# The first transfers of a two-layer transformer trunk, taken in fourths and in turn, with ScalarE as a second issuer

## The reference, cut to what matters

```python
def rmsnorm(x, g):
    y = x * lax.rsqrt(jnp.mean(x * x, axis=-1, keepdims=True) + EPS)
    return y * g

def swiglu(h, w_gate, w_up, w_down):
    return (jax.nn.silu(h @ w_gate) * (h @ w_up)) @ w_down

for i in range(DEPTH):                       # DEPTH = 2
    x = x + 0.5 * swiglu(rmsnorm(x, norm_ff1[i]), ff1_w_gate[i], ff1_w_up[i], ff1_w_down[i])
    x = x + token_mixer(rmsnorm(x, norm_mix[i]), ...)
    x = x + 0.5 * swiglu(rmsnorm(x, norm_ff2[i]), ff2_w_gate[i], ff2_w_up[i], ff2_w_down[i])
    g = jax.nn.sigmoid(rmsnorm(x, norm_ple[i]) @ ple_w_gate[i])
    x = x + g * (p[i] @ ple_w_proj[i])
return rmsnorm(x, norm_final)
```

## Time and profile before

| | |
|---|---|
| median of 3 runs | 1175.71 us (1175.65 to 1175.8) |
| the profiled execution's own time | 1175.59 us |
| its span, from the first to the last instruction | 1173.7 us |
| TensorE busy | 1166.6 us, 99% of the span |
| VectorE, ScalarE, GpSimd busy | 820.7, 609.7, 117.1 us |
| DMA | 218.87 MB, mean 186 GB/s |

### The profile page before, as it was taken

The page is one execution under the profiler, slowest core; times in us unless marked ns, Lnnn a source line. Parts: engine busy times, 40 slices in busy tenths (PEclk is TensorE's granted clock), DMA queues, the critical chain, the costliest instruction groups (busy, mean ns, idle before and its releaser), DMA issues.

```text
span 1173.7 us, 24027 instructions
## 1 busy us (share of the span) xinstructions
PE 1166.6 (99%) x10518; PEld 1142.9 (97%) x10518; DVE 820.7 (70%) x936; ACT 609.7 (52%) x688; POOL 117.1 (10%) x130
## 2 busy tenths in 40 slices
PE   9999999999999999999999999999999999999998
PEld 9999999999999999999999999999899999999998
DVE  6866545697978766655786665458799787666556
ACT  6544445555745644444764443446466555444445
POOL 2000001011512000001110000100134020000011
PEclk9999999999999999999999999999999999999999
DMA  8655555545445555555556555554644456555551
GB/s 294 232 202 190 189 206 169 193 150 200 154 145 194 200 193 201 192 187 198 191 175 224 183 203 189 183 214 140 220 145 146 143 204 211 205 182 202 192 180 37
DMA packets 33528, 218.87 MB, mean 186 GB/s; under 512 B 5200, under 2 KB 6544, under 8 KB 7440
## 3 DMA queue, kind: packets, MB, share of 16 engines
q1 hardware_dynamic: 32992, 216.82, 53.3%
q10 hardware_dynamic: 432, 0.52, 0.1%
HBM read 216.15 MB, written 1.05 MB: 185 GB/s over the span
## 4 chain that ended last, share of the span: by engine, by line
PE 98%; DMA 1%; DVE 1%; ACT 0%; SPq 0%; issue 0%; DVEq 0%
PE psum L409 32%; PE psum L410 31%; PE psum L411 31%; PE psum L691 1%; PE psum L670 1%; DMA x_all<-in_x 1%; PE psum L543 0%; PE psum L604 0%; PE psum L654 0%; PE psum L725 0%; DVE gates L1801 0%; PE psum L736 0%; PE psum L639 0%; PE psum L759 0%; DVE hB_lo L1769 0%; PE psum L586 0%
## 5 line engine op out<-in xcount | busy, mean ns | idle before, releaser
L1309 DVE TENSOR_TENSOR w_lo<-raw,w_hi 128x2048 fp32r<-128x2048 f32 x200 | 457.9, 2292 | 218.2 <-ACT w_hi L905 218.0
L905 ACT ACTIVATE w_hi<-raw 128x2048 fp32r<-128x2048 f32 x201 | 385.2, 1916 | 352.3 <-PE psum L411 347.7
L409 PE MATMUL psum<-hA_hi,w_hi 128*128 128x256 f32 x1360 | 377.6, 278 | 0.0
L410 PE MATMUL psum<-hA_hi,w_lo 128*128 128x256 f32 x1360 | 375.7, 276 | 0.0
L411 PE MATMUL psum<-hA_lo,w_hi 128*128 128x256 f32 x1360 | 375.7, 276 | 0.0
L409 PEld LDWEIGHTS psum<-hA_hi,w_hi 128*128 128x128 f32 x1360 | 255.4, 188 | 2.7 <-issue 2.7
L410 PEld LDWEIGHTS psum<-hA_hi,w_lo 128*128 128x128 f32 x1360 | 255.4, 188 | 0.0
L411 PEld LDWEIGHTS psum<-hA_lo,w_hi 128*128 128x128 f32 x1360 | 255.3, 188 | 0.0
L409 PE MATMUL psum<-hB_hi,w_hi 128*128 128x256 f32 x832 | 229.9, 276 | 0.6 <-DVE w_lo L1777 0.6
L410 PE MATMUL psum<-hB_hi,w_lo 128*128 128x256 f32 x832 | 229.7, 276 | 0.0
L411 PE MATMUL psum<-hB_lo,w_hi 128*128 128x256 f32 x832 | 229.7, 276 | 0.0
(11 more groups left out here) (207 smaller groups left out, 1241.4 us busy)
## 6 DMA issues: line engine op xcount, KB each, us to landing
raw<-in_weights SPq DMA_DIRECT2D x203, 1024.0 KB, 4.9
raw<-in_weights SPq DMA_DIRECT2D x2, 512.0 KB, 6.3
x_all<-in_x SPq DMA_DIRECT2D x1, 520.0 KB, 3.6
x_all<-in_x SPq DMA_DIRECT2D x1, 512.0 KB, 6.3
relu<-in_p SPq DMA_DIRECT2D x2, 256.0 KB, 5.1
consts<-in_consts SPq DMA_DIRECT2D x1, 384.0 KB, 5.1
out<-gates ACTq DMA_DIRECT2D x2, 192.0 KB, 2.3
out<-gates SPq DMA_DIRECT2D x2, 192.0 KB, 2.3
```

What stands on the lines that cost most here:

```text
L409: pe.matmul(o, lh, rh, start=start, stop=False)
L410: pe.matmul(o, ll, rh, start=False, stop=False)
L905: act.activation(w_hi[:, s, :], raw[:, s, :], ACT.Copy).then_inc(hi_ready[s], 1)
L1309: dve.tensor_tensor(w_lo[:, s, :], raw[:, s, :], w_hi[:, s, :].bitcast(F32), ALU.subtract).then_inc(lo_ready[s], 1)
```

## The change

x is loaded in fourths (two tiles each), and so are chunks 0 and 1; chunk 2 is loaded in halves. SyncE issues x's and chunk 1's fourths in turn, then chunk 2's halves. ScalarE issues the four pieces of chunk 0, ahead of its first activation. All four engines take the fourths in turn: of each fourth first x, then chunk 0's piece, then chunk 1's, and on ScalarE the squares of that pair behind them (of the last fourth behind chunk 2). TensorE takes chunk 0's and chunk 1's fourth m, then m + 1; chunk 2's products run by halves of k, into banks 5 and 6. The sum over the partitions, `mean_everywhere`, moves from ahead of chunk 3's products to behind its first 12. `WARM` goes from 18 to 11. Later FFNs keep their code, moved into `chunks_in_pieces`.

```diff
-X_HALVES = ((0, HEAD_WORDS + 4 * T), (HEAD_WORDS + 4 * T, HEAD_WORDS + 8 * T))
-WARM = 18
+X_FOURTHS = tuple((HEAD_WORDS * (i > 0) + 2 * T * i, HEAD_WORDS + 2 * T * (i + 1)) for i in range(4))
+WARM = 11
...
+            for i in range(4):
+                part = slice(*X_FOURTHS[i])
+                sp.dma_start(x_all[:, part], a["x"][:, part]).then_inc(x_landed[i], 16)
+                sp.dma_start(raw[:, 1, piece(i)], a["weights"][1, :, piece(i)]).then_inc(piece_landed[1][i] if i < 3 else landed[1], 16)
             for i in range(2):
-                part = slice(*X_HALVES[i])
-                sp.dma_start(x_all[:, part], a["x"][:, part]).then_inc(x_landed[i], 16)
                 half = slice(1024 * i, 1024 * i + 1024)
-                sp.dma_start(raw[:, 0, half], a["weights"][0, :, half]).then_inc(landed[0] if i else half_landed, 16)
-            chunk(0, 1)
-            chunk(0, 2)
+                sp.dma_start(raw[:, 2, half], a["weights"][2, :, half]).then_inc(landed[2] if i else half_landed, 16)
...
+                    if q == 3 and L + f == 0:
+                        by_columns(s, b, h, (0,), range(4))
+                        mean_everywhere(L, k, 4)
+                        by_columns(s, b, h, (0,), range(4, 8))
...
+            def first_chunks(h):
+                for m in range(4):
+                    if m < 3:
+                        pe.wait_ge(piece_lo, m + 1)
+                    else:
+                        operands(0, 0)
+                    pe.wait_ge(h_ready, of_norm(0, 0, m + 1))
+                    for c in range(2):
+                        mm = pairs(0, 0, h, c, (2 * m, 2 * m + 1))
+                    if m == 3:
+                        mm.then_inc(chunk_done[0], 1)
+                    if m < 3:
+                        pe.wait_ge(next_lo, m + 1)
+                    else:
+                        operands(0, 1)
+                    for c in range(2):
+                        mm = pairs(1, 2, h, c, (2 * m, 2 * m + 1))
+                mm.then_inc(chunk_done[1], 1)
+
+            def third_chunk(h):
+                for i in range(2):
+                    if i:
+                        operands(0, 2)
+                    else:
+                        pe.wait_ge(half_lo, 1)
+                    for c in range(2):
+                        mm = pairs(2, THIRD_BANKS, h, c, range(4 * i, 4 * i + 4))
+                mm.then_inc(chunk_done[2], 1)
...
+            for i in range(4):
+                act.dma_start(raw[:, 0, piece(i)], a["weights"][0, :, piece(i)]).then_inc(piece_landed[0][i] if i < 3 else landed[0], 16)
             act.wait_ge(half_ready, 1)
             act.activation(rsum[:, 0, :], half_neg[:, 0:2], ACT.Copy)
+            for m in range(4):
+                act.wait_ge(x_landed[m], 16)
+                for c in (2 * m, 2 * m + 1):
+                    ins = act.activation(hB[0][:, c, :], x[:, c, :], ACT.Copy, scale=first_gains[:, c:c + 1])
+                ins.then_inc(h_hi_ready, 1)
+                act.wait_ge(piece_landed[0][m] if m < 3 else landed[0], 16)
+                act.activation(w_hi[:, 0, piece(m)], raw[:, 0, piece(m)], ACT.Copy).then_inc(piece_hi if m < 3 else hi_ready[0], 1)
+                act.wait_ge(piece_landed[1][m] if m < 3 else landed[1], 16)
+                act.activation(w_hi[:, 1, piece(m)], raw[:, 1, piece(m)], ACT.Copy).then_inc(next_hi if m < 3 else hi_ready[1], 1)
+                if m < 3:
+                    squares(0, 0, m)
             for i in range(2):
...
+                half = slice(1024 * i, 1024 * i + 1024)
+                act.wait_ge(landed[2] if i else half_landed, 16)
+                act.activation(w_hi[:, 2, half], raw[:, 2, half], ACT.Copy).then_inc(hi_ready[2] if i else half_hi, 1)
             squares(0, 0, 3)
```

More of the change, by code:

```diff
@@ L224, in hybrid_trunk @@
         masks_landed = sem("masks_landed")
-        x_landed = [sem(f"x_landed{i}") for i in range(2)]
+        x_landed = [sem(f"x_landed{i}") for i in range(4)]
         layer_landed = sem("layer_landed")
@@ L489, in ffn @@
                 mm.then_inc(chunk_done[s], 1)
[L490 to L518, removed]
-                                       hid[0][:, k, :], hid[1][:, k, :], k == 0, k == 21)
-                        if k == 21 and m < 3:
-                            mm.then_inc(acc_ready, 1)
-                    mm.then_inc(chunk_done[s], 1)
+            def first_chunks(h):
[11 more added lines that the diff above has]
+                        pe.wait_ge(next_lo, m + 1)
+                    else:
+                        operands(0, 1)
+                    for c in range(2):
+                        mm = pairs(1, 2, h, c, (2 * m, 2 * m + 1))
+                mm.then_inc(chunk_done[1], 1)
@@ L1383, in ffn @@
                     chunk_products(L, n)
-                    dve.tensor_tensor(gate_sum, products(2 * g), both(rb), ALU.mult).then_inc(gate_scaled, 1)
+                    dve.tensor_tensor(gate_sum, high(THIRD_BANKS) if L + f == 0 and g == 1 else products(2 * g), both(rb), ALU.mult
+                                      ).then_inc(gate_scaled, 1)
                     if g:
@@ L1779, in _ @@
-            for i in range(4):
-                if i < 3:
-                    dve.wait_ge(next_hi, i + 1)
+            for m in range(4):
+                dve.wait_ge(x_landed[m], 16)
+                dve.wait_ge(h_hi_ready, of_norm(0, 0, m + 1))
+                for c in (2 * m, 2 * m + 1):
+                    ins = dve.scalar_tensor_tensor(out=hB[1][:, c, :], in0=x[:, c, :], scalar=first_gains[:, c:c + 1],
+                                                   in1=hB[0][:, c, :].bitcast(F32), op0=ALU.mult, op1=ALU.subtract)
+                ins.then_inc(h_ready, 1)
+                if m < 3:
+                    dve.wait_ge(piece_hi, m + 1)
+                else:
+                    dve.wait_ge(hi_ready[0], 1)
+                dve.tensor_tensor(w_lo[:, 0, piece(m)], raw[:, 0, piece(m)], w_hi[:, 0, piece(m)].bitcast(F32), ALU.subtract
+                                  ).then_inc(piece_lo if m < 3 else lo_ready[0], 1)
+                if m < 3:
+                    dve.wait_ge(next_hi, m + 1)
@@ L1782, in _ @@
                 else:
                     dve.wait_ge(hi_ready[1], 1)
-                next_piece(i)
-            split(0, 2)
+                next_piece(m)
+            for i in range(2):
+                half = slice(1024 * i, 1024 * i + 1024)
+                if i:
+                    dve.wait_ge(hi_ready[2], 1)
+                else:
+                    dve.wait_ge(half_hi, 1)
+                dve.tensor_tensor(w_lo[:, 2, half], raw[:, 2, half], w_hi[:, 2, half].bitcast(F32), ALU.subtract
+                                  ).then_inc(lo_ready[2] if i else half_lo, 1)
```

77 lines of the change are left out of this document (44 added, 33 removed).

## The result

The changed kernel takes 1177.30 us, the median of 22 runs (1176.34 to 1179.05), against 1175.72 for the kernel before (22 runs, 1175.41 to 1176.04). The ratio is 1.0014, with a 95% interval from 1.0008 to 1.0020. The forecast was 1174.7 with a range of 1173.5 to 1176.5: the sign was wrong and the time lies outside. By the bound of the prediction (0.2%, 2.35 us) the difference of 1.58 counts as within, the case that had 0.89. But the spread is new: before the runs lie within 0.6 us, after within 2.7. One execution of all that follow, the profiled one of experiment 5, ran at a granted clock of 0.75 throughout and took 1459.58 us; its time is left out everywhere.

What follows compares the result with a forecast made beforehand. TensorE bounds the kernel, busy 1166.6 of 1173.7 us. A start 0.83 earlier and gaps of 0.32 and 0.30 gone, against 0.5 of new wait and 0.1 for rounding, were put near 1.0 less: 1174.7 us, range 1173.5 to 1176.5.

Steps and rivals of the forecast that it cites:

- the case that had 0.89: Whole kernel: the time stays within 0.2% (2.35 us) of the kernel before, chance 0.89.
- its own 0.5 of waiting: Ahead of chunk 3: TensorE, free at 23.7, waits 0.5 us for `w_lo`, ready at 24.15.
- 0.83, 0.32 and 0.30 less 0.5 and 0.1: Whole sum: 0.83 earlier start, gaps of 0.32 and 0.30 gone, less 0.5 new wait and 0.1 for rounding over chunk 5.
- the chain at chunk 3: Chunk 3: load out at 15.05, landed 19.95, split 24.15, first product 24.2; 1.09 us gained at the chunk's end.
- ScalarE's four issues: Kernel start: four load issues ahead of the table load cost ScalarE 1.8 us, 2.8 at the dear end.
- I cost the supply at nothing, hidden behind ScalarE: Chunks 0 and 1: x's fourths land before ScalarE asks, so transfers add nothing; TensorE runs from 7.2 to 23.7.
- rival (a): Kernel start: ScalarE isn't held up by its issues; first product at 6.2, chunk 3 at 23.2, 1173.7 us; chance 0.14.
- The pace of the fourths: Chunks 0 and 1: per fourth TensorE needs 2.75 us, ScalarE 2.61, VectorE 2.13; chunk 0 is split at 14.95.
- Rival (c): Chunks 0, 1 and 3: fourths starved at 215 GB/s, chunk 0 done 3.15 later; 1177.8 us, 1178.7 with dear issues; chance 0.12.
- rival (b): First products: idle behind the shorter warm-up, they run at half pace, up to 2.15 us lost, 1176.4; chance 0.12.
- 5.6 is past 5.5: Warm-up: eleven matmuls end between 5.6 and 5.9, after the clock's rise at 5.5; the point against the low clock.

Runs made afterwards that it cites:

- experiment 5: The kernel before, with chunk 3's load also waiting for the end of chunk 1's split: median 1176.21 us.
- experiment 1: The changed kernel with 18 warm-up matmuls instead of 11: 1176.55 us.
- experiment 4: The changed kernel with 18 warm-up matmuls and chunk 3 landing in a buffer of its own, issued behind chunk 2 with no wait: 1175.43 us.
- experiment 4 with SyncE issuing: The kernel of experiment 4, with chunk 0's fourths issued by SyncE instead of ScalarE: 1175.70 us.

## Why the prediction was wrong

**The sum.** The forecast was a gain of 1.0 on 1175.7. Measured is a loss of 1.58. Taking the causes out one after another, in the changed kernel: 1177.30, less 0.75 for the short warm-up (experiment 1), less 1.12 for the release of chunk 3 (experiment 4), gives 1175.43. So without its two side effects the change gains 0.3 and not 1.0, and even that is not clear of the noise. The forecast without its own 0.5 of waiting would have been 1174.2; the 1.2 from there to 1175.43 is about what the two paragraphs on the supply and the pace find, 0.67 and 0.54, a sum and not an experiment. The forecast's own sum was loose as well: 0.83, 0.32 and 0.30 less 0.5 and 0.1 are 0.85, and 1.0 is what the chain at chunk 3 gave, 1.09 less 0.1.

**ScalarE's four issues: right.** 1.83 against 1.8, the table load at 3.12 against 3.1, the first tile at 4.52 against 4.6. No draining of 1.4 us appears here either: the next activation follows the 1.28 of the table load at once, against what the Trainium skill says in ScalarE: Activation LUTs, What ACT_TABLE_LOAD costs.

**The supply, "I cost the supply at nothing, hidden behind ScalarE": this step failed first.** I checked x's second fourth, 1.3 MB in, and not chunk 0's first piece, for which ScalarE was ready at about 5.4. It landed at 6.44 (issued at 1.25, 5.19 on the way). I had even written the condition in rival (a), that ScalarE "needs w's piece by 4.5 also", and did not ask when it comes. Its 0.26 MB share the engines with everything else that has been issued, at 258 to 315 GB/s from 2.5 to 6.5. The first product came at 7.87 instead of 7.2. Two of these stretches:

```profile
4.50:5.50 1.00, 1.00 (x7) 1.00 0.96 266
5.50:6.50 1.00, 0.65 (x4) 1.00 0.93 258
```

**The pace of the fourths: right in kind, late in sum.** Behind the first, ScalarE took 2.4 to 2.8 a fourth, against 2.61. TensorE ran on with two stops too short for the view of waits (0.19 from start to start at 13.54, 0.29 at 16.57, a slower matmul behind each); from 7.87 to 24.77 it took 16.90 us where the forecast's pace gives 16.36. But chunk 0 was split at 16.52 and not at 14.95. ScalarE's part of the 1.57 is 0.72 (14.60 against 13.88). The other 0.85 is VectorE: its piece of chunk 1 took 1.22 where 0.68 is usual, and two tiles of x 1.35 where 0.88 is usual, each beside an addition on GpSimd. I had VectorE and GpSimd each fit into a fourth alone, and never priced the two side by side, though the trace of the kernel before has the same piece at 1.23, beside an addition that ran from 14.30 to 15.37:

```profile
14.69 1.23 DVE L1328 TENSOR_TENSOR w_lo<-raw,w_hi 128x512 fp32r<-128x512 f32 x1
```

**Chunk 3: the mechanism right, the size wrong.** The chain I wrote down is the one that the trace shows, link by link, 1.9 us later at its end: 26.06 and not 24.2, and the "0.5 of new wait" was 1.02. Rival (c) had said that this chain decides once chunk 0 is done after 16.0, and it was done at 16.5; but (c)'s reason, fourths starved at 215 GB/s with ScalarE waiting in each of them, did not come: ScalarE waited for data in the first fourth only. The forecast had 1 us of room, the errors ahead of it summed to 1.6.

**The clock, rival (b): the short warm-up's cost is real, at 0.12.** Up to 2.15 in the prediction, 0.75 in the median, with runs from 0 to 2.5. I weighed it against the end of the warm-up ("5.6 is past 5.5"), and that margin rests on one trace: in the changed kernel's all 22 warm-up records ran at the low pace, 4.94 us in all, so the level rose only at their end or behind it. Nor did I weigh the idle time behind it, which was 1.7 and not 1.3 since the first product was late. The Trainium skill's rule (TensorE: Matmul & The Clock Gate, Part 1), that activity is what frees the clock from its throttled level, pointed this way, and the runs agree with it: 0.50 granted after 2.30 of idle time. And I took the rivals as alternatives; (b) and a late chunk 3 happened together, each smaller than its rival said.

**The chances.** "Within 0.2%" had 0.89 and came out, which is luck as far as the mechanism goes: the band was wide enough to hold a loss where a gain was forecast. The range for the time ended at 1176.5, since I let its upper end follow single rivals.

## What to carry to other kernels

A transfer split finer starts the first consumer earlier only if all that it needs in common has landed; ask of each first operand when it lands, with everything issued before and beside it. Taking two buffers in turn frees the first one at the end of the pair: whatever refills it starts that much later (here 4.7 us), so follow the refill down to the engine that wants it, and compare with the slack it had. Let a warm-up reach up to the first real product: here seven matmuls less cost 0.75 to 0.92 us in three pairs of kernels. Shortening it to fit an expected start makes the time depend on a start that isn't certain, and what one profile shows of the clock is one draw.

## What the runs showed that I had not expected

- **The clock fell behind a short gap.** After 2.30 us of idle time TensorE's first products still ran at full pace, then the granted clock was 0.50 from about 8.9 to 12.3. With 1.7 of idle time it held in the profiled execution; by the mean granted clock it fell in about four of the 22. Such a fall costs about 1 us; what makes the longest runs 2 us longer, at a mean of 0.998, no trace has caught.
- **The level first rises at very different times, and the granted clock doesn't show it.** It reads 1.00 from the start, but the pace of the warm-up changes about 4 us into one execution (experiment 4 with SyncE issuing) and only at about 7.3 in another (x and chunk 0 first, 18 warm-up matmuls), which put its first product at 8.11:

```profile
3.50:4.50 1.00, 1.00 (x8) 1.00 1.07 238
4.50:5.50 1.00, 1.00 (x11) 1.00 0.90 279
```

```profile
6.50:7.50 1.00, 1.00 (x7) 1.00 0.92 315
7.50:8.50 1.00, 1.00 (x11) 1.00 1.02 387
```

  Eleven warm-up matmuls end by 6.2. Where the rise would have come at 7, they may end ahead of it and leave the first products at the low pace; that would fit the long runs with a mean of 0.998, but it is not shown.
- **VectorE and GpSimd slow each other.** An addition of 128x256 on GpSimd took 0.74 alone and 2.33 beside a `w_lo` of 128x2048 on VectorE, whose own 2.29 stayed as it was. It ended at 24.91, 0.6 behind the `w_lo` that ran from 22.02 to 24.31, so it got next to nothing done beside it. The other way round, a VectorE piece of 0.68 took 1.22 beside an addition on GpSimd. The kernel before has the long addition too, ending 0.6 behind a `w_lo` that ran from 16.22 to 18.51, and the sums that ScalarE's squares wait for there, for 3.25 us, stand behind it:

```profile
16.78 2.33 POOL L1232 TENSOR_TENSOR total<-total,silu 128x256 f32<-128x256 f32 x1 [1.41 <-ACT silu L915]
```

- **Fourths land no sooner after their issue than halves,** but for the very first: 256 KB pieces of the weights took a median of 7.5 us (SyncE) and 6.8 us (ScalarE) to land, halves of 512 KB before 6.3, while x's first fourth took 2.6 and its first half 3.6. It looks as if the start were bound by the bytes in flight from all issues, at up to 360 GB/s until 6.5 or 7.5 us, then about 400; no run varied them alone. Why the stretch from 4.5 to 6.5 is slow in every variant (176 to 305 GB/s) stays open.
